# Sixteen convolution projection tiles moved from the even input stage into the scan, 256 tokens at a time

## What is computed

```
def short_conv_branch(pa, conv_w):
    u, gate_b, gate_c, z = jnp.split(pa, 4, axis=-1)
    cu = gate_c * u
    y = conv_w[0] * shift_prev(cu) + conv_w[1] * cu + conv_w[2] * shift_next(cu)
    return gate_b * y * jax.nn.silu(z)

def even_output(p, y, bon, conv_w, lnx_w, lnx_b, w_out):
    a_out = short_conv_branch(p[..., :A_COLS], conv_w)
    z_b = p[..., A_COLS + RWKV_SHIFT_COLS:]
    rw = head_group_norm(y, lnx_w, lnx_b) + bon
    b_out = rw.reshape(rw.shape[:2] + (RWKV_WIDTH,)) * jax.nn.silu(z_b.astype(jnp.float32))
    return jnp.concatenate([a_out, b_out.astype(p.dtype)], axis=-1) @ w_out

def rwkv7_scan(r, decay, k, v, a_vec, b_vec, s0, reverse):
    def step(S, inp):
        r_t, w_t, k_t, v_t, a_t, b_t = inp
        sa = jnp.einsum('bhij,bhj->bhi', S, a_t)
        S = S * w_t[:, :, None, :] + sa[..., None] * b_t[:, :, None, :] + v_t[..., None] * k_t[:, :, None, :]
        return S, jnp.einsum('bhij,bhj->bhi', S, r_t)
```

## Time and profile before

| | us |
|---|---|
| median of three timed runs | 3887.78 |
| lowest, highest | 3886.03, 3895.95 |
| the profiled execution | 3910.66 |
| its span in the trace | 3908.9 |
| even input stage, first product to last vector instruction | 151.7 to 658.5 |
| scan, first product to last output | 677 to 1355 |

### The profile page before, as it was taken

The page is one execution under the profiler, slowest core; times in us unless marked ns, Lnnn a source line. Parts: engine busy times, 40 slices in busy tenths (PEclk is TensorE's granted clock), DMA queues, the critical chain, the costliest instruction groups (busy, mean ns, idle before and its releaser), DMA issues. The chain is left out here.

```text
span 3908.9 us, 62397 instructions
## 1 busy us (share of the span) xinstructions
PE 3518.1 (90%) x27322; PEld 2970.7 (76%) x27322; DVE 1883.6 (48%) x2562; ACT 1165.1 (30%) x1621; POOL 352.7 (9%) x244
## 2 busy tenths in 40 slices
PE   5699997999999868989799998999565999999999
PEld 3488876999999747976599996677343788888887
DVE  5464545444444353225355553565456364646464
ACT  1344333111121132236444442343233221111111
POOL 0122221000000011221000002211000000000000
PEclk8799998656566579999899999999676999999999
DMA  8122234121211142132411103222300111111112
GB/s 327 46 93 89 83 114 146 31 67 35 67 35 40 44 157 97 44 127 83 161 48 60 60 13 124 69 65 79 116 16 17 47 48 50 48 50 48 49 48 72
DMA packets 144935, 294.45 MB, mean 75 GB/s; under 512 B 9888, under 2 KB 86816, under 8 KB 139040
## 3 DMA queue, kind: packets, MB, share of 16 engines
q1 hardware_dynamic: 127280, 219.24, 16.6%
q0 software_dynamic: 17392, 71.31, 5.4%
HBM read 211.22 MB, written 79.30 MB: 74 GB/s over the span
## 5 line engine op out<-in xcount | busy, mean ns | idle before, releaser
L60 PE MATMUL ev_ps<-h_hi,ev_w_hi 128*128 128x512 f32 (+1 forms) x792 | 289.0, 365 | 38.8 <-POOL ev_w_lo L483 37.5
L60 PE MATMUL ff_ps<-ff_h_hi,ff_w_hi 128*128 128x512 f32 x768 | 300.5, 391 | 9.2 <-DVE ff_w_lo L3198 7.5
L62 PE MATMUL ff_ps<-ff_h_hi,ff_w_lo 128*128 128x512 f32 x768 | 299.3, 390 | 0.0
L61 PE MATMUL ff_ps<-ff_h_lo,ff_w_hi 128*128 128x512 f32 x768 | 299.3, 390 | 0.0
L61 PE MATMUL ev_ps<-h_lo,ev_w_hi 128*128 128x512 f32 (+1 forms) x792 | 281.6, 356 | 0.0
L62 PE MATMUL ev_ps<-h_hi,ev_w_lo 128*128 128x512 f32 (+1 forms) x792 | 281.4, 355 | 0.0
L3198 DVE TENSOR_TENSOR ff_w_lo<-ff_w,ff_w_hi 128x1024 fp32r<-128x1024 f32 (+1 forms) x80 | 89.5, 1119 | 313.6 <-ACT ff_w_hi L3165 313.6
L60 PEld LDWEIGHTS ev_ps<-h_hi,ev_w_hi 128*128 128x128 f32 x792 | 150.8, 190 | 77.7 <-POOL ev_w_lo L483 38.7
L60 PEld LDWEIGHTS ff_ps<-ff_h_hi,ff_w_hi 128*128 128x128 f32 x768 | 144.3, 188 | 42.7 <-DVE ff_w_lo L3198 7.9
L3165 ACT ACTIVATE ff_w_hi<-ff_w 128x1024 fp32r<-128x1024 f32 (+1 forms) x80 | 77.9, 974 | 307.9 <-PE ff_ps L62 305.4
L61 PEld LDWEIGHTS ev_ps<-h_lo,ev_w_hi 128*128 128x128 f32 x792 | 151.0, 191 | 21.7 <-issue 1.7
(11 more groups left out here) (488 smaller groups left out, 8640.3 us busy)
## 6 DMA issues: line engine op xcount, KB each, us to landing
ff_w<-in_w_up SPq DMA_DIRECT2D x48, 512.0 KB, 3.3
ev_w<-in_ev_w_in POOLq DMA_DIRECT2D x33, 512.0 KB, 3.9
ada_wt<-in_ada_w POOLq DMA_DIRECT2D x12, 1024.0 KB, 8.4
ada_wt<-in_ada_w SPq DMA_DIRECT2D x12, 1024.0 KB, 8.5
ff_w<-in_w_down SPq DMA_DIRECT2D x32, 384.0 KB, 3.0
ar<-ev_ar SPq DMA_DIRECT2D x8, 1280.0 KB, 5.4
bk<-ev_bk SPq DMA_DIRECT2D x8, 1280.0 KB, 8.0
sc_ar<-ar SPq DMA_DIRECT2D x20, 512.0 KB, 6.1
```

Of the source, the lines that this page charges most:

```text
L60: nc.tensor.matmul(out, w_hi, x_hi, start=start, stop=False)
L61: nc.tensor.matmul(out, w_hi, x_lo, start=False, stop=False)
L62: return nc.tensor.matmul(out, w_lo, x_hi, start=False, stop=stop)
```

## The change

In `phase_even_inputs` the 16 tiles u, gc, gb, z and all their work on ScalarE and VectorE are taken out; KIND is now `lora` and then k, r, v, zb for each p. The small products are dealt out anew: `lora_products(i, 0)` stand in the r tile instead of the k tile, `lora_products(i, 1)` in the v tile, the bonus in the next k tile; `sw` and `ic` have a buffer for each direction; ScalarE's second sigmoids now stand ahead of `exponents(p, 0)`. SyncE stores h, high and low part, to a new DRAM tensor hT (2 x 5.2 MB) in the first two groups, behind v and zb.

In `phase_scan` the convolution branch is computed in units: five chunks c of 256 tokens, in each four channel groups p, in each the kinds u, gc, gb, z; 80 units, eight a block, always k = 0 to 7 of block n. A unit is one tile of 24 matmuls over 258 tokens (a neighbour on each side). h of a chunk is loaded to a stage (2.1 MB) and copied to h_hi and h_lo by ScalarE and VectorE. A unit's weights are loaded for each chunk anew, 80 loads of 512 KB instead of 16, through one buffer `sc_w` in the manner of `ev_w`. The units have the two banks bA for themselves; gram, turns, masks, `level_z` and, in the upper half of the bank, `level_p` now all go to bB. To make room in SBUF, ar has two buffers instead of three, bk and v one instead of two, y one; the loads are those of block n+1 instead of n+2.

```diff
-    KIND = ["lora", "zb"] + [x for p in range(4) for x in ["k", "r", "v", "u", "gc", "gb", "z"] + (["zb"] if p < 3 else [])]
+    KIND = ["lora"] + [x for p in range(4) for x in ("k", "r", "v", "zb")]
...
+                            if p < 2:
+                                sp.dma_start(g.hT[p], h[p][:].bitcast(F32)).then_inc(h_st, 16)
...
+    TOK, HW, SLOTS = 256, 258, 8
+    UNITS = [(c, p, x) for c in range(T // TOK) for p in range(4) for x in KINDS]
...
-                        if n >= 2:
-                            done(sp, "trBK", d, n - 2)
-                        sp.dma_start(bk[:, n % 2, d].rearrange("c p k t -> c (p k) t"),
+                        if n:
+                            done(sp, "trBK", d, n - 1)
+                        sp.dma_start(bk[:, d].rearrange("c p k t -> c (p k) t"),
...
+                def project(n, k):
+                    x = SLOTS * n + k
+                    c, p, kind = UNITS[x]
+                    pe.wait_ge(conv["w_lo"], x + 1)
+                    if x % PER == 0:
+                        pe.wait_ge(conv["h_hi"], c + 1)
+                        pe.wait_ge(conv["h_lo"], c + 1)
+                    if x >= 2:
+                        cb, pb, before = UNITS[x - 2]
+                        pe.wait_ge(conv[{"u": "u", "gc": "cu", "gb": "gb", "z": "z"}[before]], 4 * cb + pb + 1)
+                    for k in range(KD):
+                        last = product(nc, bA[x % 2][:, 0:HW], (w_hi[:, x % 2, k], w_lo[:, x % 2, k]), (h_hi[:, k], h_lo[:, k]), k == 0, k == KD - 1)
+                    last.then_inc(conv["done"], 1)
...
+                        project(n, 1)
                         level_z(n, 0)
                         level_p(n, 1)
+                        project(n, 2)
                     if old:
                         state_u(n - 1, 1)
                     if new:
                         level_z(n, 1)
                         level_p(n, 2)
+                        project(n, 3)
                     if old:
                         state_ys(n - 1, 1)
                     if new:
                         level_z(n, 2)
+                        project(n, 4)
                         level_p(n, 3)
+                        project(n, 5)
                         level_z(n, 3)
+                        project(n, 6)
                         last_p(n)
+                        project(n, 7)
                         last_z(n)
...
+                def weight(x):
+                    c, p, kind = UNITS[x]
+                    if x:
+                        pool.wait_ge(conv["w_lo"], x)
+                    pool.dma_start(w[:], g.ins["ev_w_in"][FIRST[kind] + p]).then_inc(conv["w_loaded"], 16)
+
+                def low_part(x):
+                    pool.wait_ge(conv["w_hi"], x + 1)
+                    if x >= 2:
+                        pool.wait_ge(conv["done"], x - 1)
+                    nc.gpsimd.tensor_tensor(w_lo[:, x % 2], w[:], w_hi[:, x % 2].bitcast(F32), ALU.subtract).then_inc(conv["w_lo"], 1)
...
+                def split_hi(x):
+                    if x < NU:
+                        act.wait_ge(conv["w_loaded"], 16 * (x + 1))
+                        if x >= 2:
+                            act.wait_ge(conv["done"], x - 1)
+                        cp(w_hi[:, x % 2], w[:]).then_inc(conv["w_hi"], 1)
...
                     if new:
+                        for k in range(4, 7):
+                            projected(n, k)
                         corner(n)
+                        projected(n, 7)
```

More of the change, by code:

```diff
@@ L855, in _ @@
                     sp.dma_start(dst[:], g.ins[src]).then_inc(consts, 16)
-                load(1)
+                sp.wait_ge(conv["cleared"], 1)
+                load_h(0)
                 for n in range(NB + 1):
@@ L859, in _ @@
                         store(n - 1)
[L860 to L861 removed]
+                    if n + 1 < NB:
+                        load(n + 1)
+                    if n % 2 == 0 and n // 2 + 1 < T // TOK:
+                        load_h(n // 2 + 1)
+                    if n < NB:
+                        store_conv(2 * n)
+                        store_conv(2 * n + 1)
                 for d in range(2):
[L863 to L864 removed]
+                    sp.wait_ge(yst[d], 16 * NB)
+                for j in range(2):
+                    sp.wait_ge(res_stored[j], 16 * NB)
             @block.tensor
@@ L1068, in _ @@
                                                 ALU.mult).then_inc(S["blocks", d], 1)
+                    for x in range(SLOTS * n + 2, min(SLOTS * n + SLOTS + 2, NU)):
+                        low_part(x)
+                        if x + 1 < NU:
+                            weight(x + 1)
             @block.vector
@@ new lines, in convolve @@
+                def convolve(n, k):
+                    x = SLOTS * n + k
+                    c, p, kind = UNITS[x]
+                    j, bank = 4 * c + p, bA[x % 2]
+                    if kind == "gc":
+                        dve.wait_ge(conv["done"], x + 1)
+                        dve.wait_ge(conv["u"], j + 1)
+                        tt(cu[:], bank[:, 0:HW], ub[:], ALU.mult).then_inc(conv["cu"], 1)
+                        edges = [cu[:, 0:1]] * (c in (0, 1)) + [cu[:, HW - 1:HW]] * (c in (0, T // TOK - 1))
+                        dve.wait_ge(conv["cu"], j + 1)
+                        for edge in edges:
+                            nc.vector.memset(edge, 0.0).then_inc(conv["edges"], 1)
+                        dve.wait_ge(conv["edges"], EDGES[j + 1])
+                        wc = [col(g, "conv_w", 4 * tap + p) for tap in range(3)]
+                        nc.vector.tensor_scalar(yb[:], cu[:, 0:TOK], wc[0], None, ALU.mult).then_inc(conv["taps"], 1)
+                        for tap in (1, 2):
+                            dve.wait_ge(conv["taps"], 3 * j + tap)
+                            stt(out=yb[:], in0=cu[:, tap:tap + TOK], scalar=wc[tap], in1=yb[:], op0=ALU.mult, op1=ALU.add).then_inc(conv["taps"], 1)
+                    if kind == "gb":
+                        dve.wait_ge(conv["done"], x + 1)
+                        dve.wait_ge(conv["taps"], 3 * j + 3)
+                        if j >= 2:
+                            dve.wait_ge(res_stored[j % 2], 16 * (j // 2))
+                        tt(res[:, j % 2], bank[:, 1:TOK + 1], yb[:], ALU.mult).then_inc(conv["gb"], 1)
+                    if kind == "z":
+                        dve.wait_ge(conv["z"], j + 1)
+                        dve.wait_ge(conv["gb"], j + 1)
+                        tt(res[:, j % 2], res[:, j % 2], sz[:], ALU.mult).then_inc(conv["out"], 1)
+                    if x % PER == PER - 1 and x + 1 < NU:
+                        take_h(c + 1)
```

317 lines of the change are left out of this document (173 added, 144 removed).

## The result

The changed kernel took 4005.86 us at the median (3993.96 to 4009.38), beside 3891.86 us for the kernel before in the same comparison: a ratio of 1.0275, with a 95% interval of 1.0224 to 1.0326. It is 2.75% slower by the means (4003.8 and 3896.6), and the medians are 114 us apart, where 14 us less was forecast and 3955 was the upper end of the range. By the medians the error is some 20 us larger: the profiled execution before was 23 us above the median that the forecast was set against, the one after is 2.7 above its own.

A forecast was written before the change was run, and what follows sets the result against it. The scan was taken as bound by TensorE, at its lower clock four fifths of the time. Even stage -180 us plus scan +166 gave -14, so 3874 us; range 3785 to 3955.

The forecast's parts named there:

- The even stage: Even input stage without the gate tiles: 74 us a group instead of 122.0, together -180 us (bounds -155 and -205).
- First block and start: Scan's first block 76 us against 47.5, +28; its start waits for h and its copy, +8.
- Floor and single banks: Scan block all high with eight units, 66.5 us; shared banks and waits add +5.5 (0 to 8).
- The third term: Scan, between a block's last unit and the next block's first: clock falls 6 us in, +5.5 a block (0 to 9).
- the first rival: Scan, between blocks: clock stays high, block 76 us, kernel 3820 us; chance 0.20.
- The fourth term: Weight staging in the scan through one buffer: needs 17.9 us against TensorE's 13.6, +4 a block (0 to +12).
- The upper bound's condition: Weight staging in the scan: +12 a block if two of these loads land in 8.0 us.
- GpSimd against VectorE: Scan: low parts on GpSimd slow VectorE additions of two SBUF tensors; 0 to 4 us a block, kept inside the range.
- the second and fourth terms: Scan blocks: single banks and waits, +5.5 us (0 to 8), and weight staging, +4 us (0 to +12).
- Staging and loads bind: Scan: weight turn of 9 us or more, gram can wait for bk; at 10 us a turn, 3942 us; chance 0.20.
- The clock stays high through the gap: Scan, between blocks: third term is 0, block 76 us, sum -68, kernel 3820 us; chance 0.20.
- The clock does not hold between units: Scan: level products and units run low, 124 us a block, about 4260 us at worst; chance 0.07.

The follow-up runs named there:

- e4_waits_out: Changed kernel with second weight staging buffer, copy of sc_P ahead of the split, level-0 sum ahead of convolution, inverse's corner ahead of last gate: 3824.56 us, ratio 0.983.
- e2_no_units: Changed kernel with the convolution branch left out of the scan (no units, weights or h; zeros stored for its result): 3788.62 us.
- e1_weights_kept: Changed kernel with only the first two weight tiles loaded and split, used by all eighty units (results wrong): 3854.04 us, ratio to before 0.989.
- e8_corner_last: e4_waits_out with both end-of-block orders, ScalarE's and VectorE's, put back as in the changed kernel: 3827.63 us.
- e3_add_first: Changed kernel with VectorE's sum of level 0 moved ahead of the convolution of the block's second unit: 3946.52 us, ratio 1.014.

## Why the prediction was wrong, point by point

**The even stage: right.** Groups 74.6 us apart (74), -177.4 us to the first gram, TensorE idle for 306.40 - 284.52 = 22 us in four groups, 5.5 each (5):

```profile
153.60:460.00 306.40, 284.52 (x1358) 0.97 0.36 141
```

The stores of h cost nothing that shows.

**First block and start: right.** +31 together (36).

**Floor and single banks: right in sum.** The forecast had 66.5 + 5.5 = 72.0 us for a block at the high clock with its bank waits; e4_waits_out, at 0.98, has 73.5. That is partly luck: busy time is 71.2, not 66.5, and idle 2.3, not 5.5. The floor took 0.60 from a stretch of 68 us where the nine blocks had 0.62, which by the same sum is 1.1 us of the 4.7; the low time left in e4_waits_out is an estimated 1.3 (2 x 0.02 x 73.5 us at the prediction's factor); what the rest is the runs don't show. The statement that the columns cost what the clock gives back is borne out, even against a kernel without them: e4_waits_out and e2_no_units are 36 us apart in their medians, of which 25.4 lie ahead of the nine blocks by the profiles, so the eight units, 23 us of products, cost about 1 us a block.

**The third term failed.** "So I let it fall 6 us into the stretch: +5.5." The clock's price was put in one place, the gap without units, and at about 9 us of low time and the first unit. Measured were 36 us of low time a block, 2 x (1 - 0.81) x 94.0. Against the block of e4_waits_out this is (755.48 - 640.54) / 9 = 12.8 us of busy time. The gap itself was judged wrongly in both directions. With short waits it costs next to nothing, as the first rival said (e4_waits_out holds 1.00 through it in seven of nine blocks). But behind a wait of 3 us it is low from end to end, 23.9 us.

**The fourth term failed with it.** "Staging needs: ... 17.9. So +4." The two waits named there came, and with nearly the size given: 25.3 / 9 = 2.8 us for sc_w_lo and 13.2 / 9 = 1.5 for sc_P, 4.3 us a block. The upper bound's condition, two slow loads, came in part. The eighth unit's load was issued among the loads of ar, bk and v (744.2 to 751.9). In time:

```profile
748.81 0.57 POOL L1081 DMA_DIRECT2D sc_w<-in_ev_w_in  x1 [0.30 <-POOL sc_w_lo L1087]
...
759.75 0.57 POOL L1081 DMA_DIRECT2D sc_w<-in_ev_w_in  x1 [0.30 <-POOL sc_w_lo L1087]
```

It needed 7.2 us from issue to split (755.97 - 748.81) and its turn took 10.9 us, not 8; the load behind it needed 5.8 (765.54 - 759.75). The error was to price a wait at its own length. I had both halves of the mechanism, waits of this size and a clock that needs the units, and did not ask what a wait does to the clock.

**Waits that I had small or not at all.** The convolution of the second unit ahead of the level addition was put at 1.2 us; it cost 3.0. Four operations stand there and one memset, and the two taps among them took 2.97 us beside GpSimd's subtraction, where the same two took 1.00 in the sixth unit:

```profile
846.63 1.00 DVE L1210 SCALAR_TENSOR_TENSOR sc_conv<-sc_cu,cols,sc_conv 128x256 f32<-128x256 f32 x2
```

This is the cost that stood in the range as 0 to 4 us for GpSimd against VectorE. It hit a place without slack. So did the gate ahead of the inverse's corner, 1.85 us at 767.45 beside a subtraction that began at 766.69, where the median gate took 0.43. Ahead of the next block's gram, the last gate and the split of h stand before the inverse's corner: 18.9 / 9 = 2.1 us, of which I had counted 1 in every second block. Together with the above the idle time is 10.1 us a block, where the second and fourth terms had 9.5. That the sum came out is luck: the waits for masks and copies in the shared banks, put at some 4 us, took 5.5 / 9 = 0.6, and the taps and the gram took what was left over. What the idle time does to the clock, 12.8 us a block, was forecast nowhere beyond the 5.5 of the third term; of the 12.5 us of error in a block that difference is 7.3, another 4.7 is the busy time that the floor had too small (71.2 against 66.5), and 0.6 is idle.

**The step from the profiled execution to the median.** "The difference of 23 us is taken as the same after" was wrong as well: it was 2.7. That is the 20 us by which the medians miss more than the spans, and no property of the change.

**The rivals.** "Staging and loads bind", the case on the other side, had the right sign and looked at the right place: a second buffer is worth 75 us. But its mechanism did not come. The turn was longer, as it asked, yet the waits for staging stayed at the forecast's 4.3 us a block, the gram did not wait for bk, and its 3942 us priced longer waits, not a clock that falls behind them; it came nearer by luck. "The clock stays high through the gap" (3820) is not what the change did, but what it could have done: 3824.6 us with the waits out. "The clock does not hold between units" was rightly small: it held between units wherever TensorE did not wait. That the throttle follows how busy TensorE is does not fit e2_no_units either, where it is busy for 629.82 of 667.5 us at 0.59, a larger share than in the changed kernel at 0.81.

The Trainium skill (TensorE: Matmul & The Clock Gate, Why this matters for your kernels) does state the rule that I left out: idle times between bursts of matmuls bring the slow level back. The runs agree with it in direction, and shorter waits than those the page warns of were enough here: in e1_weights_kept and e8_corner_last five waits of 1.5 us were followed by a low stretch and two by none, and one of 2.2 us in e4_waits_out was followed by one. Nor is the length of a wait all that counts. In e8_corner_last two low stretches of 18 and 20 us (from 1032 and 872) stand behind waits of no more than 0.7 and 0.9 us, and one of about 10 us in e4_waits_out (from 583) behind waits of 0.3, 1.0 and 0.8 us close together. What else decides stays open.

## What to carry to other kernels

Where TensorE's clock is up only because dense work is spread through small work, price each wait of a few microseconds ahead of small work as the wait plus the low stretch behind it, up to the next dense piece. Here a wait of 3.0 us cost 6.0 us a block (e3_add_first). Before adding filler work to a bound engine, list what its producers must finish ahead of each point where it has no slack, and put the filler's helpers behind that: one staging buffer more and four steps in another order turned 2.75% slower into 2.3% faster.

## What the runs showed of the hardware

- With dense units between them and waits of mostly under 1 us, the 64-row products ran at the granted clock of 1.00 for whole blocks (418 us without a break in e4_waits_out, below). Without the units the same products ran at 0.59, though TensorE was idle for only 4.2 us of 74.2; in the kernel before, at 0.62 with 1.1 of 66.7.

```profile
818.20:1236.00 417.80, 407.21 (x8771) 1.00 0.37 111
```

- Eight units a block, 1726 full products more in nine blocks, by the records of e4_waits_out and e2_no_units, left a block as long in the profiled executions (73.5 against 74.2 us), and about 1 us longer by the medians.
- A wait of 2.2 us was followed by 16.9 us at the low level in e4_waits_out (the clock fell within the wait), through a stretch that ran high in seven of the other eight blocks:

```profile
799.70:801.90 2.20, 0.08 (x2) 0.83 0.28 86
801.20:818.10 16.90, 16.28 (x144) 0.50 0.10 33
```
